# Routing in two expert layers: half of the second tile's gather products moved behind the samples' slot products, and more constant products ahead of two waits

## The chip, the cores and the metric

One of the eight cores of a Trainium2 chip runs the whole program. The time is device microseconds for one launch; the profile is a recorded execution of the same program. A lower time is better. TensorE is the matmul engine, VectorE and ScalarE work elementwise, GpSimd starts the indirect transfers, and SyncE starts the plain ones.

## The reference, cut to what matters

One inference step of a two-layer trunk over 256 prompt tokens and 64 sample tokens (8 sequences of 8), 1024 wide. Layer 0 is windowed attention beside a diagonal state-space mixer, layer 1 a gated linear recurrence beside dilated attention. After each mixer comes a hierarchical mixture of experts: RMSNorm, the best of 4 groups, the best 2 of the group's 4 experts, gated MLPs 256 wide, and a weighted sum.

```python
yp = yp + op.astype(yp.dtype)
ys = ys + os_.astype(ys.dtype)
...
yp = yp + hier_moe(rmsnorm(yp, norm_ffn[layer]), mp).astype(yp.dtype)
ys = ys + hier_moe(rmsnorm(ys, norm_ffn[layer]), mp).astype(ys.dtype)
```

The change is in the kernel's part for `hier_moe`, between the mixer's output product and the first expert pair. That part runs once in each of the two layers.

## The kernel before, in words

All arithmetic on the path is float32. The 320 tokens are three tiles: tile 0 and tile 1 of 128 prompt rows, and tile 2 with the 64 sample rows. The sixteen experts run as eight pairs; a pair takes up to 64 rows for each of its two experts.

TensorE's order is written out by hand in `_(pe)` of `moe_block`. `project` and `project_samples` are the mixer's output product of the prompt tiles (line 1424) and of the samples (line 1432). `turn_rows` (line 1443) turns a tile's rows, `logits` (line 1451) and `logits_back` (line 1460) make the router's logits. VectorE picks the experts (`choose`, lines 1876 to 1899) and `mark` (lines 1905, 1908) writes the chosen ones and raises `sel_ok`. `places` (line 1467) are small bfloat16 products that number the rows of each expert; three more like them (line 1603) sum the whole, and their end raises `pos_pe`. From these numbers VectorE's `place` (lines 1913, 1916) makes the selection `Sf` and raises `S0_ok`.

`gather_first(t, first, end)` (line 1474) gathers the first expert pair's rows by matmul: for each of eight pieces of 128 columns, tile t's rows times tile t's selection, accumulated over the three tiles in banks 2 and 3. Tile 0 goes first, tile 2 last; the last products of tile 2 raise `first_pe`. VectorE's `first_turned` (line 1843) brings the result to `xgT`, for which `up(0)` (line 1503) waits. VectorE also makes a one-hot matrix (line 1946) for the twelve index products (line 1612), from which the row lists of the other pairs come (`idx_ok`).

The other seven pairs' rows come by indirect transfers: ScalarE stores the normalised rows to `x_rows` (line 1746), and GpSimd's `gather(j)` (line 1385) fetches pair j's rows. `gather(1)` waits for the rows of all tiles, for `idx_ok` and for `first_pe` at 3. `turn(1)` (line 1485) on TensorE waits for its arrival. SyncE's loads of expert weights wait for `done` at 6 (the samples' product), and one later load in layer 0 for `first_pe` at 2.

`keep_clock_up(bank, n, 256)` (line 182) issues n constant products, identity times 256 columns, whose result nobody reads. In this part it stands ahead of the wait for `sel_ok` at 2 in both layers, and in layer 1 also ahead of `turn_rows(2)`.

VectorE's order differs between the layers: after `mark(0, 2)`, layer 0 does `place(0, 2)` and then `add(2)` (line 1818, the samples' residual); layer 1 does `add(2)` first. In both, `apply_gain(2)` (line 1830) and `mean(2)` (line 1823) follow, and ScalarE's scaling of tile 2's rows (line 1744) waits for `mean(2)`.

Of the kernel before, what the change touches and what calls it, by code (L numbers as in the profile page):

```python
# [18 lines left out]
KC = D // P  # L19
# [1158 lines left out]
def moe_block(c, x, layer, parts, items, zeroed, xnT, copies, n_copies):  # L1178
# [116 lines left out]
    with nc.Block(no_gpsimd_drain=True) as block:  # L1295
# [124 lines left out]
        def _(pe):  # L1420
# [7 lines left out]
            def project_samples(first, end):  # L1428

                for q in range(first, end):  # L1430
                    for h in range(2):
                        last = nc.tensor.matmul(c.bank[4][64 * h:64 * h + 64, :], parts[q][:, SEQ:TOK],  # L1432
                                                where[q][:, h * 512:(h + 1) * 512], start=(q == 0), stop=(q == n_parts - 1))
                if end == n_parts:
                    last.then_inc(done, 2)
# [19 lines left out]
            def logits_back(t):  # L1455

                pe.wait_ge(lt_ok, t + 1)
                if t == 2:
                    pe.wait_ge(lg_read, 1)
                nc.tensor.matmul(c.bank[6][0:ROWS[t], 32 * t:32 * t + 20], m["lgT"][:, t * P:t * P + ROWS[t]], c.fold,  # L1460
                                 start=True, stop=True).then_inc(lg_pe, 1)
# [9 lines left out]
            def gather_first(t, first=0, end=KC):  # L1471

                for q in range(first, end):
                    last = nc.tensor.matmul(c.bank[2 + q // 4][:, (q % 4) * P:(q % 4 + 1) * P], xn[0:ROWS[t], t, q * P:(q + 1) * P],
                                            m["Sf"][0:ROWS[t], t].rearrange("p e s -> p (e s)"),
                                            start=(t == 0 and q % 4 == 0), stop=(t == 2 and q % 4 == 3))
                    if t == 2 and q % 4 == 3 or t == 0 and q == KC - 1:
                        last.then_inc(first_pe, 1)
# [95 lines left out]
            project_samples(3, n_parts - 1)  # L1574
            if layer == 1:
                project_samples(n_parts - 1, n_parts)
            pe.wait_ge(tri_ok, 1)
            pe.wait_ge(sel_ok, 1)
            places((0, 1)).then_inc(pos_pe, 1)
# [15 lines left out]
                logits(2)  # L1595
                gather_first(0, 4, KC)
            logits_back(2)
            gather_first(1)
            c.keep_clock_up(c.bank[0], 2, 256)
            pe.wait_ge(sel_ok, 2)  # L1600
            places((2,))
            for u in range(3):
                last = nc.tensor.matmul(c.bank[7][:, 64:80], ones, m["sum"][:, u, :], start=(u == 0), stop=(u == 2))
            last.then_inc(pos_pe, 1)
            pe.wait_ge(S0_ok, 2)
            pe.wait_ge(xn_ok, 3)
            gather_first(2)
# [1337 lines left out]
```

## Time and profile before

| what | value |
|---|---|
| median of 3 runs | 589.94 us |
| lowest and highest | 586.92 and 590.29 us |
| the profiled execution's own time | 587.77 us |
| its span, first to last instruction | 585.7 us |
| mean granted TensorE clock in the span | 0.991 of full |

The span leaves 2.07 us of the profiled execution's time around it. In a timeline, each line has a start, a duration, engine, source line and operation, the shapes, a count, and in brackets the idle time just before with its releaser. One float32 product appears as two matmul instructions, so `x16` is eight products. Ends of matmuls are modelled and reach a little past the point at which the next one may start.

### The profile page before, as it was taken

How to read it: one execution, taken by the hardware profiler on the slowest of the kernel's cores; microseconds unless marked ns; L12 is line 12 of the kernel's file. 1: busy time of each engine (PE TensorE's matmuls, PEld its weight loads, DVE VectorE, ACT ScalarE, POOL GpSimd, SP SyncE). 2: the span in 40 equal slices, each digit the busy share in tenths (PEclk: the TensorE clock that was granted, in tenths of full speed). 3: DMA queues.
4: the chain of work that ended last, by engine and by line, in shares of the span. 5: the costliest groups of instructions: out<-in, count | busy, mean ns of one | idle time of the engine just before them, and what ended most of it. 6: DMA issues, size and time to landing. Idle time of an engine off the chain costs nothing. (4 is left out here: it accounts for less than half of the span.)

```text
span 585.7 us, 8561 instructions
## 1 busy us (share of the span) xinstructions
PE 563.7 (96%) x3450; PEld 312.8 (53%) x3450; DVE 249.4 (43%) x595; ACT 154.5 (26%) x327; POOL 79.3 (14%) x116
## 2 busy tenths in 40 slices
PE   6999999999899999999999999999999899999994
PEld 5677877543633333336977555667654543333331
DVE  6999683224741211145542615260113652221147
ACT  6142185221301011024245103254104300101113
POOL 5960700000111210000100001000000021120000
PEclk9899999999999999999999999999999999999998
DMA  8995999897899999999899997999799999999972
GB/s 336 415 346 61 214 408 384 361 397 333 327 374 412 419 421 420 376 331 398 353 426 320 416 397 281 323 338 422 308 374 418 385 376 412 421 421 419 386 249 92
DMA packets 39930, 208.95 MB, mean 357 GB/s; under 512 B 12819, under 2 KB 14547, under 8 KB 23920
## 3 DMA queue, kind: packets, MB, share of 16 engines
q1 hardware_dynamic: 30416, 169.93, 74.8%
q0 software_dynamic: 7872, 34.53, 16.2%
q10 hardware_dynamic: 1600, 3.90, 1.7%
q8 instruction: 30, 0.49, 0.3%
q14 instruction: 12, 0.10, 0.0%
HBM read 198.77 MB, written 43.74 MB: 414 GB/s over the span
## 5 line engine op out<-in xcount | busy, mean ns | idle before, releaser
L1503 PE MATMUL bank<-arena 128*64 128x512 f32 x264 | 87.0, 611 | 0.2 <-DVE arena L1843 0.2
L1503 PE MATMUL bank<-ring,arena 128*64 128x512 f32 x232 | 74.4, 598 | 0.2 <-DVE arena L1843 0.2
L2318 PE MATMUL bank<-arena,ring 128*128 128x320 f32 x256 | 71.6, 434 | 0.0
L2318 PEld LDWEIGHTS bank<-arena,ring 128*128 128x128 f32 x256 | 48.0, 190 | 21.3 <-issue 1.6
L1503 PEld LDWEIGHTS bank<-arena 128*64 128x64 f32 x264 | 24.4, 140 | 32.8 <-issue 32.7
L577 PE MATMUL bank<-xnT,ring 128*128 128x320 f32 x144 | 41.1, 448 | 0.5 <-DVE xnT L896 0.5
L1424 PE MATMUL bank<-ring,arena 128*128 128x512 f32 x92 | 40.3, 594 | 1.0 <-PEq L455 0.6
L1534 PE MATMUL bank<-arena 128*64 128x512 f32 x136 | 39.8, 594 | 0.7 <-ACT arena L1757 0.7
L1977 DVE COPY arena<-bank 128x512 f32<-128x512 f32 x14 | 9.7, 691 | 68.3 <-PE bank L1534 68.3
L1534 PE MATMUL bank<-ring,arena 128*64 128x512 f32 x120 | 36.1, 593 | 0.7 <-ACT arena L1757 0.7
L577 PEld LDWEIGHTS bank<-xnT,ring 128*128 128x128 f32 x144 | 28.0, 196 | 12.4 <-issue 1.2
L1503 PEld LDWEIGHTS bank<-ring,arena 128*64 128x64 f32 x232 | 21.2, 136 | 24.7 <-issue 24.5
L1755 ACT ACTIVATE arena<-bank 128x256 f32<-128x256 f32 x16 | 6.1, 383 | 92.6 <-PE bank L1503 92.6
L1971 DVE TENSOR_TENSOR arena<-arena,bank 128x256 f32<-128x256 f32 x16 | 6.7, 421 | 53.5 <-ACT arena L1755 53.5
L1424 PEld LDWEIGHTS bank<-ring,arena 128*128 128x128 f32 x92 | 17.2, 190 | 22.7 <-issue 22.7
L1393 POOL DMA_INDIRECT y_rows<-arena x12 | 12.1, 1005 | 110.1 <-DVE arena L1977 110.1
L1852 DVE TENSOR_TENSOR arena<-bank,small 128x512 f32<-128x512 f32 x28 | 18.0, 685 | 20.4 <-PE bank L1485 20.3
L1760 ACT COPY arena<-bank 128x512 f32<-128x512 f32 x16 | 9.4, 585 | 65.0 <-PE bank L1534 65.0
L1534 PEld LDWEIGHTS bank<-arena 128*64 128x64 f32 x136 | 12.4, 136 | 20.7 <-issue 20.1
L2374 PE MATMUL bank<-ring,arena 128*128 128x512 f32 (+1 forms) x64 | 21.2, 489 | 0.0
L1739 ACT ACTIVATE arena<-resid 128x1024 f32<-128x1024 f32 (+1 forms) x6 | 6.3, 1057 | 54.8 <-DVE resid L1818 54.8
L1534 PEld LDWEIGHTS bank<-ring,arena 128*64 128x64 f32 x120 | 11.3, 136 | 16.2 <-issue 15.7
(450 smaller groups left out, 853.7 us busy)
## 6 DMA issues: line engine op xcount, KB each, us to landing
arena<-in_w_moe SPq DMA_DIRECT2D x50, 1024.0 KB, 16.1
ring<-in_w_moe SPq DMA_DIRECT2D x44, 1024.0 KB, 15.0
arena<-in_stream_b SPq DMA_DIRECT2D x4, 2560.0 KB, 15.0
out_o_d_old<-in_cache_d_g POOLq DMA_DIRECT2D x1, 8448.0 KB, 29.8
arena<-in_stream_a SPq DMA_DIRECT2D x4, 2048.0 KB, 10.6
out_o_d_old<-in_cache_d_g POOLq DMA_DIRECT2D x1, 7680.0 KB, 40.4
out_o_d_old<-in_cache_d_g SPq DMA_DIRECT2D x1, 4608.0 KB, 37.9
ring<-in_w_out_even SPq DMA_DIRECT2D x2, 2048.0 KB, 11.7
```

The costliest lines, as they stand in the source:

```text
L577: last = nc.tensor.matmul(bank(name)[:, 0:TOK], lhs(k), c.xnT[:, k, :], start=(k == 0), stop=(k == KC - 1))
L1393: pool.indirect_dma_start(out=x["y_rows"], out_offset=bass.IndirectOffsetOnAxis(ap=scatter_idx[:, j:j + 1], axis=0), in_=yo_of(j), in_offs ...
L1424: last = nc.tensor.matmul(c.bank[2 * t + h][:, :], parts[q][:, t * P:(t + 1) * P], where[q][:, h * 512:(h + 1) * 512], start=(q == 0), sto ...
L1503: last = nc.tensor.matmul(c.bank[2 + j % 2][half, :], xgT[:, j % 2, q, half], w[i][q // 4][:, q % 4, :], start=(q == 0), stop=(q == KC - 1))
L1534: last = nc.tensor.matmul(c.bank[4 + h][half, :], hidT[:, j % 2, f, half], w[i][:, f, h * 512:(h + 1) * 512], start=(f == 0), stop=(f == 1))
L1739: nc.scalar.activation(xn[0:rows, t], c.resid[0:rows, t], ACT.Square, accum_out=c.stat[0:rows, t:t + 1]).then_inc(sq_ok, 1)
L1760: nc.scalar.copy(yo_of(j)[:, 0:512], c.bank[4][:, :]).then_inc(yo_a, 1)
L1852: v.tensor_tensor(xgT[:, j % 2, 4 * h:4 * h + 4, :], c.bank[h][:, :].rearrange("p (k r) -> p k r", k=4), c.gains[:, gain, 4 * h:4 * h + 4] ...
L1971: v.tensor_tensor(hid[:, j % 2], sg[:, j % 2], c.bank[2 + j % 2][:, FF:2 * FF], ALU.mult).then_inc(hid_ok, 1)
L1977: v.tensor_copy(yo_of(j)[:, 512:D], c.bank[5][:, :]).then_inc(yo_b, 1)
L2318: last = nc.tensor.matmul(bank(name)[:, 0:TOK], w[:, k, i * P:(i + 1) * P], xnT[:, k, :], start=(k == 0), stop=(k == KC - 1))
L2374: last = nc.tensor.matmul(bank(f"v{2 * t + n}")[:, 0:m], xnT[:, k, t * P:(t + 1) * P], wv[:, k, c0:c0 + m], start=(k == 0), stop=(k == KC ...
```

## The change

Three edits, all in `_(pe)` and so in both layers. Ahead of the first wait for `sel_ok`, two constant products are added in layer 0 and five in layer 1. Ahead of the second, the constant products go from two to four, and tile 1's gather products 4 to 7 no longer stand there. These four (eight instructions) stand behind the products that raise `pos_pe`, ahead of the wait for `S0_ok` at 2. The other engines' programs are untouched.

```diff
             if layer == 1:
                 project_samples(n_parts - 1, n_parts)
+            c.keep_clock_up(c.bank[0], 2 if layer == 0 else 5, 256)
             pe.wait_ge(tri_ok, 1)
             pe.wait_ge(sel_ok, 1)
             places((0, 1)).then_inc(pos_pe, 1)
...
             logits_back(2)
-            gather_first(1)
-            c.keep_clock_up(c.bank[0], 2, 256)
+            gather_first(1, 0, 4)
+            c.keep_clock_up(c.bank[0], 4, 256)
             pe.wait_ge(sel_ok, 2)
             places((2,))
             for u in range(3):
                 last = nc.tensor.matmul(c.bank[7][:, 64:80], ones, m["sum"][:, u, :], start=(u == 0), stop=(u == 2))
             last.then_inc(pos_pe, 1)
+            gather_first(1, 4, KC)
             pe.wait_ge(S0_ok, 2)
             pe.wait_ge(xn_ok, 3)
             gather_first(2)
```

## Rows read from the trace of the kernel before

**Rows 1.** The page: busy time of each engine, share of the span, instructions.

```profile
PE 563.7 (96%) x3450; PEld 312.8 (53%) x3450; DVE 249.4 (43%) x595; ACT 154.5 (26%) x327; POOL 79.3 (14%) x116
```

**Rows 2.** Waits of PE, layer 1's routing to the end: total, times, longest.

```profile
PE bank L1467 <- DVE arena L1908: 1.2, 1, 1.2
PE bank L1474 <- DVE arena L1916: 0.8, 1, 0.8
...
PE bank L1485 <- DMA arena<-x_rows,arena: 0.2, 1, 0.2
```

**Rows 3.** Timeline of PE in layer 0's routing.

```profile
142.52 3.65 PE L1432 MATMUL bank<-ring,arena 128*64 128x512 f32 x16
146.74 0.22 PE L1467 MATMUL bank<-arena 128*128 128x16 bf16 x3 [0.57 <-DVE arena L1908]
...
152.00 2.05 PE L1474 MATMUL bank<-arena 128*128 128x128 f32 x16
153.89 1.03 PE L182 MATMUL bank<-resid,ident 128*128 128x256 f32 x4
154.93 0.23 PE L1467 MATMUL bank<-arena 128*128 128x16 bf16 x3
155.01 0.22 PE L1603 MATMUL bank<-arena 128*128 128x16 bf16 x3
155.99 2.05 PE L1474 MATMUL bank<-arena 64*128 64x128 f32 x16 [0.76 <-DVE arena L1916]
```

**Rows 4.** Timeline of PE: the first pair's up product in layer 0.

```profile
158.60 8.66 PE L1503 MATMUL bank<-arena 128*64 128x512 f32 x32 [0.15 <-DVE arena L1843]
```

**Rows 5.** Windows: stretch, length, busy by engine, PEclk, DMA share, GB/s.

```profile
158.00:160.00 2.00, 1.84 (x17) 0.94 (x18) 1.86 (x10) 0.00 (x0) 0.00 (x0) 0.60 1.00 422
160.00:162.00 2.00, 2.00 (x8) 0.59 (x6) 0.50 (x3) 0.00 (x0) 1.66 (x3) 0.55 1.05 442
```

**Rows 6.** Timeline of PE at full clock: two neighbouring 512-column instructions.

```profile
174.00 0.59 PE L1503 MATMUL bank<-ring,arena 128*64 128x512 f32 x1
...
174.43 0.59 PE L1503 MATMUL bank<-ring,arena 128*64 128x512 f32 x1
```

**Rows 7.** Line 182's weight loads in layer 1: duration in ns, first and last start.

```profile
L182 PEld LDWEIGHTS bank<-resid,ident x4: 187/190/190, 459.6 to 460.1; 128*128 128x128 f32 x4
```

**Rows 8.** Timeline of DVE in layer 0's routing.

```profile
154.70 0.17 DVE L1908 TENSOR_TENSOR arena<-arena 64x16 bf16<-64x16 f32 x1
...
157.77 1.28 DVE L1843 TENSOR_TENSOR arena<-bank,small 128x512 f32<-128x512 f32 x2
```

**Rows 9.** Timeline of PE in layer 1's routing.

```profile
455.55 2.80 PE L1432 MATMUL bank<-ring,arena 128*64 128x512 f32 x12
459.51 0.22 PE L1467 MATMUL bank<-arena 128*128 128x16 bf16 x3 [1.17 <-DVE arena L1908]
459.59 1.11 PE L182 MATMUL bank<-resid,ident 128*128 128x256 f32 x4
460.74 0.71 PE L1443 MATMUL bank<-ident,resid 64*128 64x64 f32 x8
...
470.77 7.09 PE L1503 MATMUL bank<-ring,arena 128*64 128x512 f32 x32 [0.15 <-DVE arena L1843]
```

**Rows 10.** The chain that ended last, in layer 1's routing: start, length, what.

```profile
459.99 0.70 DVE resid L1818
...
462.23 0.17 DVE stat L1823
...
463.61 8.48 DMA x_rows<-arena
...
472.95 5.05 DMA arena<-x_rows,arena
```

**Rows 11.** Line 1385 around the first indirect gather of layer 0.

```profile
L1385 POOL DMA_INDIRECT arena<-x_rows,arena x1: 1120/1120/1120, 160.2 to 160.2; - x1
...
DMA to landing us min/median/max: 4.3/4.3/4.3
```

## The prediction

> **What bounds the kernel now.** I read the page first: TensorE (PE) is busy for 96% of the span and no other engine for half of it [rows 1]. Then PE's list of waits: from layer 1's routing to the end of the program the longest is 1.2 us, and all that concern this change are three waits of 1.2, 0.8 and 0.2 us [rows 2]. So PE's order sets the time, and whatever lengthens it ahead of the first expert pair is paid, unless it falls into one of these waits. Third, the timelines of PE and VectorE (DVE) around them, for the room that each wait leaves. Fourth, the windows with the granted clock: from 158 to 162 us it stood at 0.60 and 0.55 of full [rows 5], that is mostly at the lower level of 1.2 GHz, just after PE had waited 0.76 us and then run sixteen products of 64 rows [rows 3]. The first up product, 32 instructions, took 8.66 us there [rows 4] and 7.09 us in layer 1 at full clock [rows 9]. The difference, 1.57 us, is what that low stretch cost, since PE's order is the path.
>
> The change fills waits with work. Its question is whether 1.57 us comes back, against what the fillers cost where they overflow their wait.
>
> **Price of the fillers.** No row shows a stream of more than two constant products. One product of 256 columns is two instructions. At full clock, 512-column instructions start 0.43 us apart [rows 6], so 256 columns are 0.215 and a product is 0.43 us. Groups differ by a start-up: the two products of rows 9 last 1.11 and those of rows 3 last 1.03, so I add 0.08 once. Two products: 0.86 + 0.08 = 0.94 us; five: 2.15 + 0.08 = 2.23. The bound above is 1.11 / 2 = 0.55 each. The bound below is one weight load, 0.19 [rows 7]. I take 0.43, because the columns must be streamed.
>
> The Trainium skill (TensorE: Matmul & The Clock Gate, Back-to-back issue gap) has a spacing of N/2.4 + 2.5 ns for a warm matmul of N columns, 109 ns at N = 256. This trace disagrees for float32: 0.43 us at 512 columns, about twice the rule's 216 ns, and two instructions per product. By the page all seven products of the first waits would be hidden, and the sum further down would end near 588.5 us.
>
> **Layer 0, first wait.** The samples' product ends at 142.52 + 3.65 = 146.17; neighbouring groups show that the next may start about 0.07 earlier. With the 0.57 of idle time, the room is 0.64 us [rows 3]. Two products need 0.94, so `places` starts 0.94 - 0.64 = 0.30 us later. Behind it on PE stand the samples' last output product, and with it `done`, `add(2)`, the turning of tile 2, its logits and its choice. All of these move by 0.30. SyncE's late weight loads wait for `done` too and start 0.30 later; PE has no wait for a weight load in rows 2, so I count nothing for them. Bounds: 0 with products of 0.19 (0.38 < 0.64), and 0.47 with 0.55.
>
> **Layer 0, second wait.** Eight of the sixteen gather instructions go: half of 153.89 - 152.00 = 1.89, so 0.95 [rows 3]. Two products come: 0.86. Net -0.09, and it gains nothing: `places` of tile 2 starts at 154.93, right behind `mark`'s end at 154.70 + 0.17 = 154.87 [rows 8], so DVE sets this start. Zero. If products cost 0.55, it is +0.15, of which PE's own slack (153.89 + 0.86 = 154.75 against 154.87) covers 0.12.
>
> **Layer 0, third wait.** The slot products end at 155.23, and the gather of tile 2 waited 0.76 for `Sf` [rows 3]; the room is 0.76 + 0.07 = 0.83. The moved half is 0.95 + 0.08 = 1.03. It overflows by 0.20. Behind it stand tile 2's gather, the index products and `up(0)`. `up(0)` had its own 0.15 us of waiting for `first_turned` [rows 4, 8], whose inputs arrive early enough for the first half, so 0.05 reaches it. DVE's chain from `pos_pe` on is not delayed, because the moved products stand behind `pos_pe`. Bounds: 0 and 0.20.
>
> Layer 0 pays 0.30 + 0.05 = 0.35 us (0 to 0.7). The first indirect gather starts at 160.2 and lands 4.3 later, at 164.5 [rows 11]. `turn(1)` needs it after `up(0)`; with `up(0)` 1.57 shorter it comes at 158.60 + 0.35 + 7.02 = 165.97 (7.02 is 7.09 less the 0.07), against a landing of 164.8. That stays hidden, by 1.2 us.
>
> **Layer 1, first wait.** The room is 1.17 + 0.07 = 1.24 us [rows 9]. Five products need 2.23, so `places` starts 0.99 later, at 460.50, and ends at 460.72. DVE does not mind: it is in `add(2)` until 459.99 + 0.70 = 460.69 [rows 10]. But PE does. Its two old constant products now follow at 460.58 and take 0.94, so `turn_rows(2)` starts at 461.52 instead of 460.74, which is 0.78 late. Before, these two filled the wait for `add(2)`; that wait is now used twice. Tile 2's gain, logits, choice and slots follow by 0.78. The second and third waits are as in layer 0: 0 and 0.05. `up(0)` starts about 0.83 late. Bounds: 0.05 with cheap products (0.95 < 1.24), 1.4 at 0.55.
>
> The second path in layer 1 is the one that the chain shows: `mean(2)` at 462.23, tile 2's rows to memory, 8.48 us in flight, then the gather, 5.05 us, landing at 478.00 [rows 10]. `mean(2)` stands behind `apply_gain(2)` on DVE, which needs the turned tile. The turned halves come near 461.9 and 462.2, a gain of some 0.4 us follows each (an estimate from the 0.70 us of `add(2)`'s half, which has twice the columns), and `mean(2)` starts near 462.67, 0.44 late, which puts the landing at 478.44. PE had 0.2 us of waiting at `turn(1)` [rows 2], 0.26 with the overlap, so it comes there at 0.83 - 0.26 = 0.57 late, 478.6, behind the landing. Layer 1 pays 0.57 us (0 to 1.2).
>
> **The sum.** 0.35 + 0.57 = +0.92 for the fillers, -1.57 for the low-clock stretch if it does not come, together -0.65. The profiled execution would go from 587.77 to 587.1. The median of the runs is 2.17 above it, and I subtract the same difference there: 589.94 - 0.65 = 589.3 us.
>
> Will the stretch go? What PE did ahead of the fall was tiny slot products, 0.76 us of nothing and products with half the rows [rows 3]. Afterwards a full-height half gather stands in place of the idle time. The same routing in layer 1 stood at full clock with the same waits, at another moment; so the fall is not certain in each execution before, and each of the two layers can have it. I take one fall saved per execution as the likeliest, since the trace shows one there.
>
> **The rivals.**
>
> Two falls saved. PE has almost no waits, so a spread of 3.37 us between the runs before is about two low stretches of 1.57, and the median's 2.17 above the profiled execution is more than one. If the median execution has one more fall than the profiled one, in layer 1's routing, the time is 589.94 + 0.92 - 3.14 = 587.7 us. Against it: the trace shows none in layer 1.
>
> Slower: the fillers are paid and no fall is saved. The place is `turn_rows(2)` in layer 1 (0.57) and the first wait in layer 0 (0.35). It gives 589.94 + 0.92 = 590.9 us, and 591.8 at 0.55 a product. It decides from the point where the median run has less than 0.92 / 1.57 = 0.6 of a fall to save. For it: layer 1 shows none, and the phase at which the clock falls is not in the program. To be slower by over 1% it would need 5.9 us, several times every filler together.
>
> Everything hidden: products as cheap as their weight load. Then only the fall and the 0.10 of the third waits count: 589.94 - 1.57 + 0.10 = 588.5 us. Against it stands the spacing in rows 6. It is where the page's rule named above would lead as well.
>
> The change does nothing for the clock and nothing for the order: the difference is lost in the spread, 589.9 us.
>
> **How the numbers follow.** One fall saved, fillers paid: 0.38, at 589.3. Two or more saved: 0.22, at 587.7, down to 586.2 with a third. None saved: 0.25, at 590.9, up to 591.8. All hidden: 0.05, at 588.5. Nothing: 0.05, at 589.9. Something not in these rows: 0.05. The range reaches from near the third fall, 586.3, to short of the upper price, 591.5. One per cent is 5.9 us and about what a measurement of this kernel can tell from no change: every case above lies within it, so 0.94 for within 1%. Faster by over 1% needs four falls saved, 0.03; slower by over 1% has no mechanism here, 0.03.
>
> **What would show it.** In the changed kernel: line 182 with ten more 256-column instructions in layer 1 ahead of line 1467, at 0.215 us each, and no idle time before it; `turn_rows(2)` in layer 1 0.8 us later behind the end of the samples' product (5.2 us after its start at 455.55 before, 6.0 after); the idle time before line 1474's 64-row group gone, with that group 0.2 us later against line 1603; full clock over the first up products of both layers, 7.1 us each. The prediction is wrong if a low stretch still falls on layer 0's up product, if `turn_rows(2)` is not late, or if `turn(1)` waits longer than 0.5 us for its rows.

## The result

The change made the kernel slower: 591.41 us at the median of 20 runs against 588.52 us for the kernel before in runs beside them, a ratio of 1.0051 with a 95% interval of 1.0031 to 1.0071. That is 3.0 us more, inside the 1% that I had called no change, but clear of its own interval and against the sign of the forecast (-0.65 us). The profiled execution took 594.02 us, its span is 591.9 us.

What each part did to TensorE's order in layer 0 is in the timeline of PE after (start, length, as before):

```profile
142.51 3.65 PE L1432 MATMUL bank<-ring,arena 128*64 128x512 f32 x16
146.10 1.13 PE L182 MATMUL bank<-resid,ident 128*128 128x256 f32 x4
147.06 0.22 PE L1467 MATMUL bank<-arena 128*128 128x16 bf16 x3
...
153.32 1.89 PE L182 MATMUL bank<-resid,ident 128*128 128x256 f32 x8
155.25 0.23 PE L1467 MATMUL bank<-arena 128*128 128x16 bf16 x3
155.34 0.22 PE L1604 MATMUL bank<-arena 128*128 128x16 bf16 x3
155.42 3.12 PE L1474 MATMUL bank<-arena 128*128 128x128 f32 x24
...
158.93 7.09 PE L1503 MATMUL bank<-arena 128*64 128x512 f32 x32
166.37 1.09 PE L1485 MATMUL bank<-ident,arena 128*128 128x128 f32 x8 [0.36 <-DMA arena<-x_rows,arena]
```

Against [rows 3, 4]: `places` is 0.32 us later, the half gather runs into tile 2's gather without idle time, `up(0)` starts 0.33 late, and it takes 7.09 us instead of 8.66. The windows show why: full clock where it had been 0.60 and 0.55 [rows 5].

```profile
158.00:160.00 2.00, 1.99 (x23) 1.28 (x24) 1.93 (x9) 0.00 (x0) 0.00 (x0) 1.00 1.05 442
160.00:162.00 2.00, 2.00 (x13) 0.73 (x10) 0.76 (x5) 0.00 (x0) 1.33 (x3) 1.00 0.99 418
```

The loss stands elsewhere. PE's waits from 155 to 285 us, after and then before, where the same wait has line 1674:

```profile
PE bank L1676 <- ACT arena L1787: 3.2, 1, 3.2
...
PE bank L1503 <- issue: 0.5, 1, 0.5
...
PE bank L1485 <- DMA arena<-x_rows,arena: 0.4, 1, 0.4
```

```profile
PE bank L1674 <- ACT arena L1785: 0.6, 1, 0.6
```

Line 1676 is the turning of the next layer's first tile, at the end of layer 0's experts. TensorE came there sooner and waited 3.2 us instead of 0.6. The turning itself started later, at 270.05 instead of 267.81. And behind this wait the clock fell (windows after; the number behind POOL's is the granted clock):

```profile
270.00:272.00 2.00, 1.95 (x12) 1.13 (x12) 1.26 (x3) 1.44 (x3) 0.00 (x0) 0.79 0.69 295
272.00:274.00 2.00, 2.00 (x9) 1.05 (x6) 0.97 (x3) 0.00 (x0) 0.00 (x0) 0.50 0.29 123
```

So the low stretch was not saved. It moved from `up(0)` to behind the turning, and there no wait absorbed it. By the samples' product in layer 1 (459.48 against 455.55) the program was 3.9 us behind: 2.2 from the later turning, and 1.7 from the part that followed, which holds the slow stretch. In layer 1 the fillers cost what was forecast: `turn_rows(2)` started 6.11 us behind the samples' product (5.19 before, [rows 9]), `up(0)` 0.87 us late and `turn(1)` 0.62 late. The last 1.7 us of the 6.2 between the two spans came at the end of layer 1's experts, with its own `y_rows` loads; this execution lies 2.6 us over its median, so the two spans overstate the difference.

What is late at the end of layer 0 is a transfer. VectorE adds the other pairs' rows (`y_rows`) to tile 0 and tile 1 before the turning, and it waits for SyncE's loads of them. Its timeline after, and then before:

```profile
258.95 2.60 DVE L2024 SCALAR_TENSOR_TENSOR resid<-ring,arena,resid 128x1024 f32<-128x1024 f32 x2 [5.10 <-DMA ring<-y_rows]
263.18 2.60 DVE L2024 SCALAR_TENSOR_TENSOR resid<-ring,arena,resid 128x1024 f32<-128x1024 f32 x2 [1.63 <-DMA ring<-y_rows]
```

```profile
256.60 2.60 DVE L2022 SCALAR_TENSOR_TENSOR resid<-ring,arena,resid 128x1024 f32<-128x1024 f32 x2 [2.43 <-DMA ring<-y_rows]
260.93 2.61 DVE L2022 SCALAR_TENSOR_TENSOR resid<-ring,arena,resid 128x1024 f32<-128x1024 f32 x2 [1.73 <-DMA ring<-y_rows]
```

SyncE issued these loads at 245.26, 1.9 us sooner than before (247.19), and yet the second landed at 263.09 instead of 260.84. In both traces the turning starts 6.96 to 6.97 us after this landing (270.05 and 267.81).

### The profile page after: what moved, and what is told of

It reads as the page before. It is cut to its first block and busy times, and to the rows that moved or that the text cites. A ratio compares the mean times of both kernels' runs of the same rounds, so it can differ in the third digit from the quotient of the medians.

```text
span 591.9 us, 8605 instructions
## 1 busy us (share of the span) xinstructions
PE 568.1 (96%) x3472; PEld 317.8 (54%) x3472; DVE 249.7 (42%) x595; ACT 154.6 (26%) x327; POOL 84.0 (14%) x116
## 5 line engine op out<-in xcount | busy, mean ns | idle before, releaser
L1503 PE MATMUL bank<-arena 128*64 128x512 f32 x264 | 85.6, 598 | 0.5 <-issue 0.5
L1534 PE MATMUL bank<-arena 128*64 128x512 f32 x136 | 39.8, 594 | 0.7 <-ACT arena L1759 0.7
```

Source lines behind the costliest of these rows:

```text
L1503: last = nc.tensor.matmul(c.bank[2 + j % 2][half, :], xgT[:, j % 2, q, half], w[i][q // 4][:, q % 4, :], start=(q == 0), stop=(q == KC - 1))
L1534: last = nc.tensor.matmul(c.bank[4 + h][half, :], hidT[:, j % 2, f, half], w[i][:, f, h * 512:(h + 1) * 512], start=(f == 0), stop=(f == 1))
```

## The experiments

Each ratio is against the kernel before in runs beside it, with its 95% interval; each profile is one execution. Two theories were tested: that whatever TensorE does late in routing is paid (the path theory of the prediction), and that the end of layer 0's experts is set by the stream of expert weights and the `y_rows` loads behind it (the stream theory).

**The parts, one by one.**

```diff
+            if layer == 0:
+                c.keep_clock_up(c.bank[0], 2, 256)
             pe.wait_ge(tri_ok, 1)
```

> Only the two constant products ahead of the first wait in layer 0. Path theory (whatever TensorE does late in routing is paid): up(0) of layer 0 starts 0.3 us late and the program ends 0.3 us late, +0.3 us. Stream theory (the end of layer 0's experts is set by the expert weights' stream and the y_rows loads behind it, and this stream starts with done): the samples' weight loads start 0.3 us late, the y_rows loads land 0.3 us late whatever TensorE does, +0.3 us; a low-clock stretch that is saved ahead of up(0) would not show in the end of the layer, but as a longer wait at line 1674. The two differ if the clock is full at up(0): the path theory has the whole program 1.3 us faster, the stream theory 0.3 us slower.

Measured: 1.0011 (0.9992 to 1.003), about +0.6 us and not told apart from nothing. In its trace the low stretch still stood at `up(0)` (8.41 us), so this run could not separate the two theories.

```diff
+            if layer == 1:
+                c.keep_clock_up(c.bank[0], 5, 256)
             pe.wait_ge(tri_ok, 1)
```

> Only the five constant products ahead of the first wait in layer 1. Path theory: turn_rows(2) of layer 1 0.8 us late against the end of the samples' product, up(0) 0.8 late, turn(1) 0.55 late, and the end 0.6 to 0.8 us late. Stream theory: the same places late, but the end is late by 0.6 to 0.8 only if the y_rows loads at the end of layer 1 start as much later; layer 0 as before.

Measured: 1.0020 (0.9999 to 1.004), +1.2 us. In its trace `turn_rows(2)` starts 6.11 us behind the samples' product, 0.92 late, as in the whole change.

```diff
-            gather_first(1)
-            c.keep_clock_up(c.bank[0], 2, 256)
+            gather_first(1, 0, 4)
+            c.keep_clock_up(c.bank[0], 4, 256)
...
             last.then_inc(pos_pe, 1)
+            gather_first(1, 4, KC)
```

> Only the moved half gather and the four products ahead of the second wait, in both layers. Path theory: up(0) 0.05 us late in each layer, and 1.6 us saved in each execution whose clock would have fallen there: between -1.5 and +0.1 us. Stream theory: the saving in layer 0 does not reach the end; TensorE reaches line 1674 earlier, waits there up to 2 us longer, and its clock falls there instead, so 0 to +1.5 us.

Measured: 1.0036 (1.0008 to 1.0063), +2.1 us, which is outside what the path theory allows. This is the part that was to save time, and it costs most. Its profile has `up(0)` at full clock, a wait of 1.9 us at the turning and the low stretch from the end of this wait on.

> The whole change once more, for a second trace and times beside the parts. If the parts add up: the sum of the three differences, near +3 us. If the 3.2 us wait at the turning of the next layer's first tile and the low stretch behind it belong to the change, both stand in this trace again; if they were an accident of one execution, the wait is near 0.6 us.

Measured, with the whole change once more: 1.0047 (1.0022 to 1.0071), +2.8 us, which agrees with the sum of the parts, 3.9, within their intervals. In this execution the wait was 0.5 us and no low stretch followed, so size and fall differ from one execution to the next; the 3.2 us of the first profile are at the high end.

**Where the later waits lose.**

```diff
-            gather_first(1)
-            c.keep_clock_up(c.bank[0], 2, 256)
+            gather_first(1, 0, 4 if layer == 0 else KC)
+            c.keep_clock_up(c.bank[0], 4 if layer == 0 else 2, 256)
...
+            if layer == 0:
+                gather_first(1, 4, KC)
```

> The moved half gather and the four products ahead of the second wait in layer 0 alone. Stream theory: up(0) of layer 0 stands at full clock (7.1 us), TensorE reaches the turning of the next layer's first tile (line 1676 of the changed kernel) 1 to 3 us too early, its clock falls there in most executions, and this one edit holds most of what all the later waits lost: +1 to +2 us. Path theory: -1.5 us where the low stretch is saved, else 0.

Measured: 1.0029 (1.0000 to 1.0058), +1.7 us. The wait was 1.6 us (264.14 to 265.79), and its windows show the fall at the end of it and behind it:

```profile
264.00:266.00 2.00, 0.35 (x3) 0.21 (x2) 1.35 (x3) 1.70 (x4) 0.00 (x0) 0.81 1.07 459
266.00:268.00 2.00, 2.00 (x10) 1.65 (x11) 0.90 (x2) 1.21 (x3) 0.00 (x0) 0.50 0.94 406
```

> The same edits in layer 1 alone. Stream theory: layer 0 is that of the kernel before, with its low stretch at up(0) and no long wait behind it; layer 1's up(0) is 0 to 0.1 us late, so 0 to +0.4 us. If the loss of the later waits sits in layer 1, +1 to +2 us here.

Measured, with the same diff for layer 1: 1.0002 (0.9975 to 1.0030). By the middle values the loss sits in layer 0; this interval alone reaches up to 1.8 us.

**Is there slack in layer 0's experts?** To the whole change, 1.8 us of constant products were added, first in the middle of the expert stage, then in the wait at its end. These are two kernels; each has one of the two fillers.

```diff
             turn_gates(0)
+            if layer == 0:
+                c.keep_clock_up(c.bank[3], 4, 256)
             up(1, 0, UP_AHEAD)
```

> The whole change, and in layer 0 four constant products (1.8 us) ahead of the second pair's up product, in the middle of the expert stage. Stream theory: TensorE's 1.8 us are swallowed by the wait for the rows at the end of layer 0, which shrinks by as much; the clock falls there less often, and the time is the same as or up to 1.5 us less than with the change alone, in spite of the added work. Path theory: 1.8 us slower than the change alone, near +4.5 us against the kernel before.

Measured: 1.0028 (1.0005 to 1.0051), against 1.0047 without them. More work on the engine that is busy for 96% of the span made the program no slower. By the medians (589.49 against 590.54 us) it was 1 us faster, but the two intervals overlap. The path theory wanted 4.5 us over the kernel before; the upper end of the interval is 3.0. In the trace there is no wait at the turning at all, and the second `y_rows` load landed at 255.54, 108.8 us behind the stretch's first weight load, where the change's took 114.8 and 111.4.

```diff
             if layer == 0:
+                c.keep_clock_up(c.bank[4], 4, 256, m["G"][1])
                 turn_next(next_norm, 0)
```

> The whole change, and in layer 0 four constant products (256 columns, 1.8 us) in the wait ahead of the turning of the next layer's first tile. Stream theory: the clock no longer falls behind that wait; the turning starts where it did, when its rows are there, and the end is 1 to 1.5 us earlier than with the change alone, so +1 to +1.8 us against the kernel before. Path theory (no slack there): the four products are paid and it is slower than the change alone, near +4.5 us.

Measured: 1.0065 (1.0038 to 1.0092), +3.8 us. The stream theory's +1 to +1.8 lies outside the interval. The path theory's +4.5 lies inside it, but its reason, no slack at the turning, does not fit the trace. There was no low stretch in its trace, but the rows landed at 262.33, TensorE still waited 1.0 us at the turning, and it also waited 1.3 us for a piece of weights in the experts:

```profile
PE bank L1503 <- issue: 1.3, 1, 1.3
PE bank L1676 <- ACT arena L1788: 1.0, 1, 1.0
```

The first line names no releaser; in both this trace (piece at 241.36, TensorE on at 241.5) and the change's (241.84 and 241.9) a weight piece landed just then. Filling the wait does not make the rows come sooner. The filler would be paid in executions in which the wait is short, but no trace here shows one, and why this kernel is slower than the change alone stays open; the two intervals overlap.

**Why an earlier issue lands later.** SyncE issues the three `y_rows` loads when the last scatter has landed. With a faster `up(0)` that is sooner, while more weight pieces are still in the queues: in the change's trace three pieces of 1 MB landed after the issue, in that of the kernel before two. The next kernels leave TensorE's order alone and hold SyncE.

```diff
+                    if layer == 0:
+                        sp.wait_ge(dn_pe, LAST)
                     rows = x["y_rows"].rearrange("(t two) d -> t (two d)", two=2)
```

> The whole change, and in layer 0 SyncE issues the y_rows loads (and the next layer's weights behind them) only when the seventh pair's down product has ended, some 3 us later than now; TensorE's order is untouched. If the loads land late because they are issued early, ahead of a queue that is still full (packets of 700 to 900 ns), they land 1 to 2 us earlier now, the wait at the turning shrinks to 0 to 1 us, and the time is 1 to 1.5 us below the change alone. If their landing is set by the weight stream ahead of them alone, they land at the same time and the time is that of the change, +2.8 us; if the issue sets it, 3 us later and +4 to +5 us.

Measured: 1.0004 (0.9975 to 1.0033), so 2.5 to 2.8 us below the change by its two ratios. It does not help in every execution: eight of the twelve runs took 586.7 to 590.4 us and four took 591.3 to 592.6. The first load, issued at 247.14, lands in 5.3 us instead of 13.7. Line 1347 after the hold, then line 1345 in the change (duration in ns, start, and time to landing):

```profile
L1347 SPq DMA_DIRECT2D ring<-y_rows x1: 327/327/327, 247.1 to 247.1; - x1
...
DMA to landing us min/median/max: 5.3/5.3/5.3
```

```profile
L1345 SPq DMA_DIRECT2D ring<-y_rows x1: 326/326/326, 245.3 to 245.3; - x1
...
DMA to landing us min/median/max: 13.7/13.7/13.7
```

The windows from 250 to 262 us say the same by rate: the DMA engines are fully busy in both, at 338 GB/s with the hold and at 236 GB/s in the change (before: 316).

```profile
250.00:262.00 12.00, 12.00 (x44) 4.19 (x41) 6.95 (x7) 3.77 (x7) 0.00 (x0) 1.00 1.02 338
```

```profile
250.00:262.00 12.00, 12.00 (x46) 4.07 (x43) 2.99 (x3) 3.32 (x6) 0.00 (x0) 1.00 1.05 236
```

By the packet records, an 8 KB packet takes 309 ns in the weight stream. In the change those from 252 us on take 580 to 920 ns (medians over stretches of 2 us), for 10 us. With the hold they stay at 309 ns until 254 and are slow, at 720 to 740 ns, for only 4 us.

> The kernel before with the same hold in layer 0. Its loads are issued some 1.5 us later than now. Early-issue theory: the landing is at most 0.5 us earlier, 0 to -0.5 us. Stream theory: the same time, within 0.3 us. Issue theory: +1.5 us.

Measured, with the hold in the kernel before: 0.9998 (0.9980 to 1.0016). No difference: it issues late already (247.78 with the hold), and TensorE does not wait at the turning.

```diff
+                if j == LAST - 2 and layer == 0:
+                    sp.wait_ge(dn_pe, LAST)
                 for item in odd_w.get(j, []):
                     c.load_item(sp, item)
```

> The whole change; the y_rows loads of layer 0 are issued early as in the change, and only the next layer's weight load behind them (IT_XR, 2 MB) is held until the seventh pair's down product has ended. If it is the early issue of the y_rows loads that makes their packets slow: landing and time as with the change alone, +2.5 to +3 us. If it is the weight load standing in the queues behind them: landing 2 us earlier and time as with both held, 0 to +0.5 us.

Measured: 1.0033 (1.0005 to 1.0062), +1.9 us, with 2.3 us of waiting at the turning. This told little, since the hold had nearly passed: the weight load went at 247.88 instead of 247.63. So it was held longer:

```diff
+                if j == LAST - 2 and layer == 0:
+                    sp.wait_ge(sum_pe, 1)
```

> The whole change, with the weight load behind the y_rows loads of layer 0 held until TensorE's first weighted sum has ended (near 253 us, when the last expert weights have landed), so 5 us later than in the change; the y_rows loads are issued early as in the change. If the early issue of the y_rows loads is what slows them: packets of 700 to 900 ns again, the second load lands no earlier, and +2.5 to +3 us or more. If the weight load in the queues behind them is: packets near 310 ns, landing 2 us earlier, and 0 to +0.8 us.

Measured: 1.0047 (1.0021 to 1.0073), +2.8 us, with the weight load issued at 252.48. The first `y_rows` load, issued at 244.50, took 11.5 us, the rate from 250 to 262 us was 272 GB/s, and TensorE waited 2.0 us at the turning. So holding the load behind gains nothing. What the first hold did beyond this was to issue the `y_rows` loads themselves later, and that is what gained.

Over the sixteen traces, counted from the first of the late weight loads (line 135): seven issued `y_rows` by 97 us, and the second load landed at 111.4 to 115.1, mean 113.1. Eight others issued at 98.9 to 100.8 and it landed at 108.8 to 112.8, mean 110.8; the one between (the first experiment, issued at 98.0) landed at 110.6. The two groups overlap, so this is a difference of means and not of every execution.

**A version that beats both.** The later waits in layer 0 alone, with the hold:

> The moved half gather and the four products in layer 0 alone, with the same hold. Early-issue theory: the 1.5 us saved at up(0) come through at last in part, and it is the fastest kernel, -0.5 to -1 us against the kernel before. Stream theory: +2 us as without the hold. Issue theory: +3 to +4 us.

Measured: 0.9978 (0.9958 to 0.9997), -1.3 us. Its trace has layer 0's `up(0)` at full clock and no wait at the turning. The one low stretch in the routing stands on layer 1's `up(0)` (8.78 us), where this kernel has the old order.

> The moved half gather and the four products in layer 0 alone, with the y_rows loads held, once more: if it is really faster than the kernel before, -0.5 to -1.5 us again and its second y_rows load lands within 111.5 us of the first late weight issue.

Measured: 0.9967 (0.9947 to 0.9987), 586.84 us against 588.69. The saving at `up(0)` reaches the end at last, 1.3 to 1.9 us. The first late weight load was issued at 146.76 and the second `y_rows` load landed at 257.76, 111.0 us later, within the 111.5 that were expected. TensorE waited 0.4 us at the turning.

## Why the prediction was wrong

- **The step that failed: "The difference, 1.57 us, is what that low stretch cost, since PE's order is the path".** At the end of layer 0's experts a second path is as long as TensorE's: the `y_rows` loads. In all nine traces in which TensorE waited at the turning, it started 6.96 or 6.97 us after the second load had landed. In four of the five traces with the old order there was no wait, but that point lay only 0.0, 0.9, 1.3 and 1.5 us ahead of the turning; in the fifth, the kernel before, TensorE waited for it 0.6 us. So even with the rows landing as before, 1.57 us could come back in part at most. And they did not land as before: issued sooner, they landed later. The prediction argued from PE's waits from layer 1's routing on [rows 2]. It left out layer 0's end, where the 0.6 us at line 1674 was the sign that something else was as long there, and it has no term for the `y_rows` loads. With the old order the longest wait there was 0.6 us; with the new one and no hold of any load or filler it was 0.5 to 3.2.
- **What the loss consists of** (an estimate from the traces, one execution each). From `up(0)` to the turning took 109.2 us on average in the six traces with the new order that have no filler and do not hold `y_rows`, and 108.6 in the four with the old order and no hold, although `up(0)` itself was 1.3 to 1.6 us shorter. From the turning to layer 1's samples' product took 190.2 us on average in the five traces with the fall behind the turning and 188.0 in the eleven without. So the later rows took back the saving and 0.6 us more, and the fall costs 2.2 us where it comes. The kernel with the filler at the turning does not fit: no fall in its trace, and +3.8 us.
- **"PE has no wait for a weight load in rows 2, so I count nothing for them": not safe in layer 0.** The traces of the change, of the kernel with the filler at the turning and of layer 0's later waits with the hold (the first time) have such a wait there, 0.5, 1.3 and 0.4 us. What it cost in time was not measured.
- **The low stretch goes: right, and of no use.** It stood on layer 0's `up(0)` in all five traces with the old order and in none of the eleven with the new one. But the change's mean granted clock over its runs was no higher (0.991 in 32 runs, 0.991 to 0.992 in the kernel before), so on average as much time passed at the low clock as before, elsewhere.
- **The signs named in the prediction did not catch it.** No low stretch fell on layer 0's `up(0)`, `turn_rows(2)` was late as forecast, and `turn(1)` waited 0.36 us, under 0.5. All of them stand ahead of the place where the time was lost.
- **The nearest rival was near in part by luck.** "No fall is saved", at 590.9 us and a chance of 0.25, came within 0.5 us of 591.41. But it starts from 589.94, the median of three runs, and over 20 runs the kernel before has 588.52. As a difference it says +0.9 and not +3.0, and it names no cause at the end of layer 0.
- **The Trainium skill** (TensorE: Matmul & The Clock Gate, "Why this matters for your kernels") warns of idle gaps of PE as what brings the low clock back. The traces agree that the low clock goes with idle time, but 0.76 us of it beside products with half the rows went with it before [rows 3, 5]; after, it was 1.6 to 3.2 us of waiting. What the rule leaves open, and what decided here, is whether the engine is the bound at the place that is filled.
- **Layer 0's fillers: right.** 0.30 + 0.05 us was forecast, and `up(0)` was 0.33 late; all of it came from the first wait. The gather's landing was missed: 4.3 us was taken over and it took 5.8, so `turn(1)` waited 0.36 us where I had it hidden by 1.2.
- **Layer 1's fillers: right in the trace.** 0.78, 0.83 and 0.57 us were forecast for `turn_rows(2)`, `up(0)` and `turn(1)`; 0.92, 0.87 and 0.62 were measured. `mean(2)` was 0.60 late, not 0.44.
- **A product at 0.43 us: right.** Two held TensorE from 146.10 to 147.06, 0.96 us against 0.94, and five in layer 1 from 462.21 to 464.47, 2.26 against 2.23. The rival with every filler hidden is out, and with it the page's spacing.

Not settled: why `y_rows` packets are slow for longer when they are issued while more weight pieces are in the queues. The traces show that they are, and for how long; the loads are the same three with the same bytes, and holding the load behind them changed nothing. As for the clock behind the turning, all five traces that waited 1.6 us or more there had the fall and none of those with 1.0 or less had it; no experiment took the fall away and left the wait.

## What to carry to other kernels

An engine that is busy for 96% of the span is not the bound in every stage. Before time saved on it is counted, follow it to the next place where it waits, however short that wait is now, and ask what sets the other side. A low-clock stretch is worth removing only where the engine has no slack behind it; removed ahead of a wait, it can lengthen that wait by as much, and here the low clock then came back behind it in five of seven traces. And a load that is issued sooner into full queues can land later: hold it, and measure.

## What the runs showed of the hardware that I had not expected

- Three loads of rows that scatters had just written had slow 8 KB packets (580 to 920 ns against 309) for 10 us in the change and, issued 1.9 us later, for 4 us with the hold. The first load landed in 8.9 to 14.3 us in the seven traces that issued it early and in 5.2 to 9.4 us in the other nine. In the change and with the hold the DMA engines were fully busy from 250 to 262 us, at 236 and 338 GB/s.
- The 1.8 us of added constant products in the expert stage cost nothing that could be seen: 589.49 us against 590.54 without them, with overlapping intervals.
- One SyncE issue of such a load took 1485 ns in the change, where its other two took 326 and 432 ns. Six more of the sixteen traces have one issue of 912 to 1622 ns.
